# First loads of a two-block transformer kernel dealt to two DMA queues, and one split placed ahead of two sums

## The chip, the core and the metric

The kernel runs on one core of a Trainium2 chip: TensorE (PE) for matmuls, VectorE (DVE), ScalarE (ACT), GpSimd (POOL), SyncE (SP), and 16 DMA engines that the queues of SP, ACT and POOL share. The metric is device time in microseconds (us), the median of several executions; one further execution was profiled.

## The reference

256 tokens of width 1024 pass through a first block (modulated FFN, token mixer, modulated FFN) and a second block of two layers. What matters here is the first block's opening:

```python
cond = jax.nn.silu(c)                                  # c: 1024 values
mod = cond @ w_ada[l] + b_ada[l]                       # w_ada: 1024 x 9216
sh1, sc1, gt1, sh2, sc2, gt2, sh3, sc3, gt3 = jnp.split(mod, 9, axis=-1)
u = modulate(rmsnorm(h, g_norm_ffn1[l]), sh1, sc1)     # x * (1 + sc1) + sh1
h = h + 0.5 * gt1 * swiglu(u, w_ffn1_in[l], w_ffn1_out[l])
```

So before the first real matmul the kernel needs `x`, the shift columns of `w_ada` (block 0, 1024 x 1024), its scale columns (block 1, the same size), a bias and a gain vector, and the first unit of `w_ffn1_in`. All is float32; matmuls take each operand as a sum of two float16 parts (`hi` + `lo`), three products each.

## The kernel before

**Weights.** Weights of the matmuls come in units of 1 MiB (128 partitions x 2048 floats) into a ring `raw` of six slots. ACT makes `whi` of a unit (L444), DVE makes `wlo` (L469, `lo_part`), PE then multiplies (L750). Units 0 and 1 are the two halves of the first FFN chunk (its a and its b side). SP issues the units (`load`, L561); from unit 2 on it first waits until block 0 of the modulation is used up, since slots 2 to 5 hold that block until then.

**The opening.** Each modulation block comes in four pieces of 1 MiB, `j` = 0 to 3, of two row tiles each. DVE multiplies the pieces 0, 1 and 2 by `cond` and sums them (`ada_first_sums`, six sums, L2343 and L2345); PE takes piece 3 directly (`ada_direct`, L1054) and adds DVE's sums over partitions (`ada_ones`, L1060). ACT issues block 0 (pieces in the order 0, 3, 1, 2), the two halves of `x` (L1858) and, when `cond` is made, block 1 (L542). SP issues `c`, an identity matrix, a 204 KB table of constants (`small`, L565), 17 vectors of gains and biases (L575) and two rows of `b_ada` (L578), then positions, sinks and a router bias (L579 to L582), and units 0 and 1. The constants' table, the 17 vectors and the two bias rows count on one semaphore, `stack_in`; each counts 16, so 20 loads make 320.

**Who waits.** PE works in program order: `c` transposed (L1045), `ada_direct(0)`, then a wait for all 20 loads of `stack_in`, the transposes of the vectors and biases (L1067, L1068), then a wait for DVE's six sums, `ada_ones(0)` (L1060), 12 matmuls on zeros that keep the engine busy (`stay_warm`, L902), the transposes of the normalised `x` (L882), `ada_direct(1)` with two such matmuls before each pair, five more, `ada_ones(1)` (first 4 columns after sum 12, the other 4 after sum 13), five more, four matmuls that open the output banks (L822), five fillers (L853), and only then the first product of unit 0 (L750). ACT waits for `stack_in` too, before the mean squares of `x` (L1739). DVE waits for PE's two vector transposes between the sums of block 0 and those of block 1. After the sums of block 1 DVE makes `wlo` of unit 0, then the shift and scale columns (L2488 to L2495), from which ACT and DVE make `uhi` and `ulo`, the other operand of unit 0.

The order of all this is written out by hand; each queue issues in program order.

Of the kernel before, what the change touches and what calls it, by code (L numbers as in the profile page):

```python
# [27 lines left out]
D = 1024  # L28
# [5 lines left out]
RING = 6  # L34
# [6 lines left out]
HALF = 512  # L41
# [133 lines left out]
def build(nc, a, out):  # L175
    small_d, b1_d, b2_d = a["const_small"], a["const_block1"], a["const_block2"]
    with ExitStack() as ctx:
        def sb(name, shape, dt=F32):
            return ctx.enter_context(nc.sbuf_tensor(name, shape, dt))

        def sem(name):
            return ctx.enter_context(nc.semaphore(name))


        raw = sb("raw", [P, RING, UNIT])
# [164 lines left out]
        raw_in = [sem(f"raw_in{i}") for i in range(RING)]  # L350
        hi_made, lo_made, used = sem("hi_made"), sem("lo_made"), sem("used")
# [80 lines left out]
        def size(u):  # L432
            return sizes.get(u.c, UNIT) if isinstance(u.turn, int) and u.turn == 0 else UNIT
# [26 lines left out]
        def lo_part(dve, u):  # L460

            if isinstance(u.turn, int) and u.c + RING * u.turn >= U_END:
                return
            if ada_index(u) is not None:
                ada_unit_sums(dve, u, ada_index(u))
                return
            n = size(u)
            dve.wait_ge(hi_made, u.count(1))
            dve.scalar_tensor_tensor(out=wlo[:, u.slot, 0:n], in0=raw[:, u.slot, 0:n], scalar=SW,  # L469
                                     in1=whi[:, u.slot, 0:n], op0=ALU.mult, op1=ALU.subtract).then_inc(lo_made, 1)  # L470
# [51 lines left out]
        ffn1 = Phase(U_FFN1, 0, FFN_CHUNKS, ffn_src(a["w_ffn1_in"][0], a["w_ffn1_out"][0]))  # L522
# [10 lines left out]
        def ada_index(u):  # L533

            if isinstance(u.turn, int) and u.turn == 0 and u.c - U_MIX in ADA_POS:
                return ADA_POS.index(u.c - U_MIX)
            return None

        def ada_first(eng, b):

            for j in (0, 3, 1, 2):
                eng.dma_start(first_w[b][j], w_ada[:, 2 * j:2 * j + 2, b * D:(b + 1) * D]).then_inc(ada_in[b][j], 16)  # L542

        def ada_block(eng, b):

# [8 lines left out]
        @block.sync  # L554
        def _(sp):
            def load(u, src):
                if isinstance(u.turn, int) and u.c + RING * u.turn >= U_END:
                    return
                sp.wait_ge(lo_made, u.count(1 - RING))
                k, n = src.shape[1], src.shape[2]  # L560
                sp.dma_start(raw[:, u.slot, 0:k * n].rearrange("p (k n) -> p k n", k=k), src).then_inc(raw_in[u.slot], 16)  # L561

            sp.dma_start(cstack[0:8, :], a["c"][0].rearrange("(r n) -> r n", n=P)).then_inc(const_in, 16)
            sp.dma_start(small[:, 0:P], small_d[:, 0:P]).then_inc(const_in, 16)
            sp.dma_start(small[:, P:C_SMALL], small_d[:, P:C_SMALL]).then_inc(stack_in, 16)  # L565
            rows = [(V_G1, a["g_norm_ffn1"][0]), (V_G2, a["g_norm_mix"][0]),
                    (V_G3, a["g_norm_ffn2"][0]), (V_GF, a["g_final"])]
            for l in range(LAYERS):
                rows += [(V_LN1G + 8 * l, a["ln1_g_2"][l]), (V_LN1B + 8 * l, a["ln1_b_2"][l]),
                         (V_LN2G + 8 * l, a["ln2_g_2"][l]), (V_LN2B + 8 * l, a["ln2_b_2"][l]),  # L570
                         (V_QN + 3 * l, a["mla_q_norm_w_2"][l]), (V_KVN + 2 * l, a["mla_kv_norm_w_2"][l])]
            rows.append((V_PS, a["pool_scale"][0]))
            for r, v in rows:
                v = v.rearrange("(r n) -> r n", n=P)
                sp.dma_start(vstack[r:r + v.shape[0], :], v).then_inc(stack_in, 16)  # L575
            for r, m in ((B_SH1, M_SH1), (B_SH3, M_SH3)):
                v = a["b_ada"][0, m:m + 2 * D].rearrange("(r n) -> r n", n=P)
                sp.dma_start(bstack[r:r + 16, :], v).then_inc(stack_in, 16)  # L578
            sp.dma_start(posi, a["positions"][0].partition_broadcast(P)).then_inc(rows_in, 16)  # L579
            sp.dma_start(sinks[:, :], a["swa_sinks_2"].rearrange("l h -> (l h)").partition_broadcast(P)).then_inc(rows_in, 16)  # L580

            sp.dma_start(rbias[:, :], a["router_bias_2"].partition_broadcast(P)).then_inc(rows_in, 16)  # L582

            def phase(ph):
                load(Unit(ph.u0), ph.src("a", 0))
                load(Unit(ph.u0 + 1), ph.src("b", 0))
                if ph is ffn1:
                    sp.wait_ge(ada_sum, 6)
                    sp.wait_ge(ada_pe, 1)

                def step(c, u, par):
                    load(u, ph.src("a", c))
                    load(u + 1, ph.src("b", c))
                    load(u + 2, ph.src("o", c - 1))
                steps(sp, ph, step)
                load(Unit(ph.u0 + 3 * ph.n - 1), ph.src("o", ph.n - 1))

            phase(ffn1)
            for i in range(N_MIX):
                load(Unit(U_MIX + i), sources[U_MIX + i])  # L600
            phase(ffn2)
            for l in range(LAYERS):
                for i in range(N_LMIX):
                    load(Unit(U_L + N_L * l + i), sources[U_L + N_L * l + i])
                units, wholes = moe_units(l)

                def load_whole(c):
                    i = WHOLE.index(c)
                    if i >= 2:
                        sp.wait_ge(whole_used, N_WHOLE * l + i - 1)  # L610
                    sp.dma_start(whole[i % 2].rearrange("p (k n) -> p k n", k=2), wholes[c]).then_inc(whole_in[i % 2], 16)

                for i, src in enumerate(units):
                    if i == 4:
                        sp.wait_ge(ret_t, l + 1)
                        sp.wait_ge(p_made, 4 + 12 * (l + 1))
                        load_whole(WHOLE[0])
                        sp.wait_ge(ret_o, 4 * (l + 1))
                        load_whole(WHOLE[1])
                    load(Unit(U_L + N_L * l + N_LMIX + i), src)  # L620
                    for c in WHOLE[2:]:
                        if MOE_ORDER[i] == ("in", c + 2, 1):
                            load_whole(c)
                for c in WHOLE[2:]:
                    if c + 2 >= EXPERTS:
                        load_whole(c)
            for t in range(TT):
                for hf in range(2):
                    c = slice(hf * HALF, (hf + 1) * HALF)
                    sp.wait_ge(x_new, 12 + 2 * t + hf + 1)  # L630
                    sp.dma_start(out[0, t * P:(t + 1) * P, c], x[:, t, c]).then_inc(out_done, 16)
            sp.wait_ge(out_done, 64)
# [1090 lines left out]
        def _(act):  # L1723
# [129 lines left out]
                act.activation(gate_sig[i], ps[:, 5 + i % 2, :], ACT.Copy, scale=1.0 / S).then_inc(proj_out, 1)  # L1853


            ada_first(act, 0)
            for t in range(TT):
                act.dma_start(x[:, t, :], a["x"][0, t * P:(t + 1) * P, :]).then_inc(x_in, 16)  # L1858
            act.wait_ge(vec_t, 1)
            act.activation(cond[:, :], ps[:, 3, 0:8], ACT.Silu).then_inc(cond_made, 1)  # L1860
            ada_first(act, 1)
            act.wait_ge(used, RING)
            act.wait_ge(stack_in, 16 * 20)
            rms_first()
# [15 lines left out]
            for i in range(10):  # L1880
                u = Unit(U_MIX + IN1_POS[i])
# [360 lines left out]
        def _(dve):  # L2242
# [89 lines left out]
            def ada_first_sums(b, cuts, ks=range(6)):  # L2332

                for k in ks:
                    if k % 2 == 0:
                        dve.wait_ge(ada_in[b][k // 2], 16)
                    edges = cuts if k == 5 else (0, D)
                    if k:
                        dve.wait_ge(ada_sum, 6 * b + k)
                    for c0, c1 in zip(edges, edges[1:]):  # L2340
                        v, w = acc1[:, b * D + c0:b * D + c1], first_w[b][k // 2][:, k % 2, c0:c1]
                        if k == 0:
                            ins = dve.tensor_scalar(v, w, cond[:, 0:1], None, ALU.mult)  # L2343
                        else:
                            ins = dve.scalar_tensor_tensor(out=v, in0=w, scalar=cond[:, k:k + 1], in1=v,  # L2345
                                                           op0=ALU.mult, op1=ALU.add)
                        ins.then_inc(ada_sum, 1)
# [127 lines left out]
                n_step[0] += 2  # L2475
            ada_first_sums(1, (0, HALF, D), range(2))
            rms_xn(0)
            ada_first_sums(1, (0, HALF, D), range(2, 6))
            lo_part(dve, Unit(0))

            def mod_columns(i, ps_sh, ps_sc, g):

# [498 lines left out]
```

## Time and profile before

| | |
|---|---|
| median of 3 runs | 1118.47 us (1117.57 to 1119.99) |
| profiled execution | 1117.76 us, span 1116.0 us |
| PE busy | 1077.0 us, 97% of the span |
| DVE / ACT / POOL busy | 78% / 57% / 8% |
| chain that ended last | PE 81%, DVE 10%, ACT 4%, DMA 3% |
| DMA in the first four slices of 27.9 us | 340, 370, 371, 373 GB/s, busy tenths 9 9 9 9 |
| PE in the first slice | 6 tenths; 9 tenths in all others but the last (6) |

The span runs from the first instruction to the last; the profiled execution's own time has 1.76 us around it. The chain is followed back from the last instruction: a share in it is time that something really waited for. Busy time alone says little: PE's first slice holds fillers too.

### The profile page before, as it was taken

To read this page: it belongs to the slowest core of one execution; us is meant where nothing else is said; L and a number is where in the kernel's file an instruction comes from. 1 tells how busy PE (TensorE), PEld (TensorE's weight loads), DVE (VectorE), ACT (ScalarE), POOL (GpSimd) and SP (SyncE) were. 2 spreads that over 40 slices of the span, in tenths; PEclk is the share of its full clock that TensorE was granted. 3 is DMA by queue.
4 is the path that set the end of the run, shared out by engine and by line. 5 is a ranking of instruction groups with operands and counts; after the bars stand their busy time and mean duration, and the time that the engine had idled before them with its cause. 6 is when DMAs were issued, how large, how long until landed. Compare 5 with 4: busy or idle time off the path is not lost.

```text
span 1116.0 us, 24969 instructions
## 1 busy us (share of the span) xinstructions
PE 1077.0 (97%) x10736; PEld 819.0 (73%) x10736; DVE 874.7 (78%) x1130; ACT 633.1 (57%) x792; POOL 90.5 (8%) x104
## 2 busy tenths in 40 slices
PE   6999999999999999999999999999999999999996
PEld 5677777688788577777778785877758877597773
DVE  4789699788787885554667967999966886799994
ACT  1544344463466554444367555877755755687771
POOL 1114621043000110000000000000000000000000
PEclk9899999999999999999999999999999999999998
DMA  9999799754556578554546226499993523579981
GB/s 340 370 371 373 278 316 359 247 177 160 189 187 229 195 254 305 194 184 167 175 143 237 94 77 231 184 378 416 414 315 107 183 89 108 222 263 396 416 363 39
DMA packets 134717, 271.94 MB, mean 244 GB/s; under 512 B 9428, under 2 KB 98104, under 8 KB 126296
## 3 DMA queue, kind: packets, MB, share of 16 engines
q1 hardware_dynamic: 124248, 231.79, 58.1%
q0 software_dynamic: 7904, 29.25, 7.3%
q10 hardware_dynamic: 2464, 9.44, 2.2%
q8 instruction: 77, 1.26, 0.5%
q14 instruction: 24, 0.20, 0.0%
HBM read 269.41 MB, written 1.05 MB: 242 GB/s over the span
## 4 chain that ended last, share of the span: by engine, by line
PE 81%; DVE 10%; ACT 4%; DMA 3%; issue 2%; ACTq 0%; DVEq 0%; SPq 0%
PE ps L750 67%; PE ps L1625 3%; DVE wlo L469 3%; DMA area<-in_w_ada_dram 2%; PE ps L1673 1%; PE ps L892 1%; PE ps L902 1%; DVE area L2841 1%; PE ps L910 1%; PE ps L1278 1%; PE ps L1247 1%; PE ps L1087 1%; DVE bnst L2282 1%; ACT area L1776 1%; PE ps L1308 1%
## 5 line engine op out<-in xcount | busy, mean ns | idle before, releaser
L469 DVE SCALAR_TENSOR_TENSOR wlo<-raw,whi 128x2048 f16<-128x2048 f32 (+4 forms) x212 | 466.0, 2231 | 36.6 <-ACT whi L444 36.0
L444 ACT ACTIVATE whi<-raw 128x2048 f16<-128x2048 f32 (+4 forms) x212 | 385.2, 1850 | 25.8 <-DMA raw<-in_w_ffn_in_dram 10.2
L750 PE MATMUL ps<-uhi,whi 128*128 128x256 f16 (+2 forms) x1328 | 329.6, 260 | 2.2 <-DVE ulo L2308 2.0
L750 PE MATMUL ps<-uhi,wlo 128*128 128x256 f16 (+2 forms) x1328 | 329.4, 260 | 0.0
L750 PE MATMUL ps<-ulo,whi 128*128 128x256 f16 (+2 forms) x1328 | 329.4, 260 | 0.0
L750 PE MATMUL ps<-whi,hreg 128*128 128x512 f16 (+1 forms) x656 | 205.0, 381 | 0.0
L750 PE MATMUL ps<-area,whi 128*128 128x96 f16 (+2 forms) x2168 | 155.0, 210 | 0.0
L750 PEld LDWEIGHTS ps<-area,whi 128*128 128x128 f16 (+2 forms) x2168 | 145.4, 99 | 11.7 <-issue 5.6
L750 PE MATMUL ps<-area,wlo 128*128 128x96 f16 (+2 forms) x1084 | 149.4, 210 | 0.0
L750 PEld LDWEIGHTS ps<-uhi,whi 128*128 128x128 f16 (+1 forms) x1328 | 130.3, 98 | 23.5 <-issue 8.9
L750 PEld LDWEIGHTS ps<-ulo,whi 128*128 128x128 f16 (+1 forms) x1328 | 130.2, 98 | 15.6 <-issue 1.9
L750 PEld LDWEIGHTS ps<-uhi,wlo 128*128 128x128 f16 (+1 forms) x1328 | 130.1, 98 | 11.5
L750 PE MATMUL ps<-wlo,hreg 128*128 128x512 f16 (+1 forms) x328 | 124.9, 381 | 0.0
L750 PEld LDWEIGHTS ps<-whi,hreg 128*128 128x128 f16 (+1 forms) x656 | 68.9, 105 | 70.6 <-issue 3.0
L750 PEld LDWEIGHTS ps<-area,wlo 128*128 128x128 f16 (+2 forms) x1084 | 107.3, 99 | 0.0
L2359 DVE SCALAR_TENSOR_TENSOR area<-area,cond 128x512 f32 (+1 forms) x94 | 72.0, 766 | 10.7 <-DMA area<-in_w_ada_dram 7.5
L1796 ACT ACTIVATE hreg<-ps 128x512 f32<-128x512 f32 x22 | 13.2, 599 | 117.1 <-PE ps L750 117.1
L750 PEld LDWEIGHTS ps<-wlo,hreg 128*128 128x128 f16 (+1 forms) x328 | 34.5, 105 | 33.5 <-issue 2.1
L2325 DVE SCALAR_TENSOR_TENSOR hreg<-ps,hreg 128x512 f32<-128x512 f32 x22 | 15.1, 688 | 46.2 <-ACT hreg L1796 46.2
L549 POOL DMA_DIRECT2D area<-in_w_ada_dram x48 | 35.0, 729 | 161.8 <-DVE area L2359 129.6
L1798 ACT ACTIVATE hreg<-hreg 128x512 f16<-128x512 f32 x22 | 13.9, 632 | 56.2 <-DVE hreg L2325 56.2
L750 PE MATMUL ps<-whi,uhi 128*128 128x256 f16 (+2 forms) x176 | 38.8, 244 | 2.0 <-DVE ulo L2310 2.0
(358 smaller groups left out, 1324.6 us busy)
## 6 DMA issues: line engine op xcount, KB each, us to landing
raw<-in_exp_w_gate_up_dram SPq DMA_DIRECT2D x64, 1024.0 KB, 8.4
raw<-in_w_ffn_in_dram SPq DMA_DIRECT2D x44, 1024.0 KB, 7.5
raw<-in_w_in_dram SPq DMA_DIRECT2D x34, 1024.0 KB, 7.0
area<-in_w_ada_dram POOLq DMA_DIRECT2D x48, 512.0 KB, 7.1
raw<-in_w_ffn_out_dram SPq DMA_DIRECT2D x22, 1024.0 KB, 7.6
raw<-in_exp_w_down_dram SPq DMA_DIRECT2D x22, 1024.0 KB, 9.2
raw<-in_w_out_dram SPq DMA_DIRECT2D x12, 1024.0 KB, 4.9
x<-in_exp_w_down_dram SPq DMA_DIRECT2D x6, 1024.0 KB, 10.1
```

What stands on the lines that cost most here:

```text
L444: act.activation(whi[:, u.slot, 0:n], raw[:, u.slot, 0:n], ACT.Copy, scale=SW)\
L469: dve.scalar_tensor_tensor(out=wlo[:, u.slot, 0:n], in0=raw[:, u.slot, 0:n], scalar=SW, in1=whi[:, u.slot, 0:n], op0=ALU.mult, op1=ALU.sub ...
L549: eng.dma_start(aring[:, j, :, :], w_ada[:, 2 * j:2 * j + 2, c0:c0 + ADA_BLOCK]).then_inc(ada_late[j], 16)
L750: last = pe.matmul(o, st, mv, start=start and i == 0, stop=stop and i == 2, skip_group_check=True)
L892: ins = pe.transpose(ps[:, 4 + 2 * t + k // 4, (k % 4) * P:(k % 4 + 1) * P], xn[:, t, k * P:(k + 1) * P], ident)
L902: pe.matmul(ps[:, bank, :], ident16, zeros16[:, :], start=True, stop=True)
L910: pe.matmul(o, st[:, k, xs], res_one, start=k % 4 == 0 and i == 0, stop=False, skip_group_check=True)
L1625: last = pe.matmul(ps[0:SLOTS, 6 + n, :], e_whole[i % 4][:, f * SLOTS:(f + 1) * SLOTS], whole[i % 2][:, f * D + n * HALF:f * D + (n + 1) * ...
L1796: act.activation(s_act, ps[:, 4 + 2 * par, :], ACT.Silu, scale=1.0 / S).then_inc(silu_made, 1)
L1798: act.activation(hhi[:, par, :], h_f32, ACT.Copy).then_inc(h_hi, 1)
L2325: dve.scalar_tensor_tensor(out=h_f32, in0=ps[:, 5 + 2 * par, :], scalar=SX / S, in1=s_act, op0=ALU.mult, op1=ALU.mult).then_inc(h_made, 1)
L2359: ins = dve.scalar_tensor_tensor(out=v, in0=w, scalar=cond[:, k:k + 1], in1=v, op0=ALU.mult, op1=ALU.add)
```

## The change

`ada_first` takes the list of pieces to issue. Of each modulation block, pieces 0 and 1 stay on ACT, and pieces 3 and 2 go to SP. On SP, block 0's two pieces stand right behind `c` and the identity, ahead of the constants' table and the vectors; unit 0 and block 1's two pieces stand behind the bias rows and ahead of positions, sinks and router bias. Unit 1 moves from SP to ACT, behind its pieces of block 1. On DVE, `wlo` of unit 0 moves ahead of the last two sums of block 1 (the three instructions of rows 4 and 5).

```diff
-        def ada_first(eng, b):
-            for j in (0, 3, 1, 2):
+        def ada_first(eng, b, js):
+            for j in js:
                 eng.dma_start(first_w[b][j], w_ada[:, 2 * j:2 * j + 2, b * D:(b + 1) * D]).then_inc(ada_in[b][j], 16)
+        def fetch(eng, u, src):
+            k, n = src.shape[1], src.shape[2]
+            eng.dma_start(raw[:, u.slot, 0:k * n].rearrange("p (k n) -> p k n", k=k), src).then_inc(raw_in[u.slot], 16)
...
             sp.dma_start(small[:, 0:P], small_d[:, 0:P]).then_inc(const_in, 16)
+            ada_first(sp, 0, (3, 2))
             sp.dma_start(small[:, P:C_SMALL], small_d[:, P:C_SMALL]).then_inc(stack_in, 16)
...
+            load(Unit(ffn1.u0), ffn1.src("a", 0))
+            ada_first(sp, 1, (3, 2))
             sp.dma_start(posi, a["positions"][0].partition_broadcast(P)).then_inc(rows_in, 16)
...
             def phase(ph):
-                load(Unit(ph.u0), ph.src("a", 0))
-                load(Unit(ph.u0 + 1), ph.src("b", 0))
                 if ph is ffn1:
                     sp.wait_ge(ada_sum, 6)
                     sp.wait_ge(ada_pe, 1)
+                else:
+                    load(Unit(ph.u0), ph.src("a", 0))
+                    load(Unit(ph.u0 + 1), ph.src("b", 0))
...
-            ada_first(act, 0)
+            ada_first(act, 0, (0, 1))
...
-            ada_first(act, 1)
+            ada_first(act, 1, (0, 1))
+            act.wait_ge(lo_made, Unit(ffn1.u0 + 1).count(1 - RING))
+            fetch(act, Unit(ffn1.u0 + 1), ffn1.src("b", 0))
             act.wait_ge(used, RING)
             act.wait_ge(stack_in, 16 * 20)
...
-            ada_first_sums(1, (0, HALF, D), range(2, 6))
+            ada_first_sums(1, (0, HALF, D), range(2, 4))
             lo_part(dve, Unit(0))
+            ada_first_sums(1, (0, HALF, D), range(4, 6))
```

SP's queue at the program's start. In the kernel before (`hreg` takes the vectors, `raw` and `area` take weights; lines as in that kernel):

```order
L563 DMA hreg<-in_c_dram 8x128
L564 DMA small<-in_const_small_dram 128x128
L565 DMA small<-in_const_small_dram 128x408
L575 DMA hreg<-in_g_norm_ffn_dram 8x128
...
L578 DMA hreg<-in_b_ada_dram 16x128 x2
L579 DMA gt<-in_positions_dram 128x256
L580 DMA sinks<-in_swa_sinks_dram 128x12
L582 DMA rbias<-in_router_bias_dram 128x16
L561 DMA raw<-in_w_ffn_in_dram 128x8x256 x2
```

The same place in the changed kernel (its lines are numbered a few higher):

```order
L567 DMA hreg<-in_c_dram 8x128
L568 DMA small<-in_const_small_dram 128x128
L542 DMA raw<-in_w_ada_dram 128x2x1024 x2
L570 DMA small<-in_const_small_dram 128x408
L580 DMA hreg<-in_g_norm_ffn_dram 8x128
...
L583 DMA hreg<-in_b_ada_dram 16x128 x2
L547 DMA raw<-in_w_ffn_in_dram 128x8x256
L542 DMA area<-in_w_ada_dram 128x2x1024 x2
L586 DMA gt<-in_positions_dram 128x256
L587 DMA sinks<-in_swa_sinks_dram 128x12
L589 DMA rbias<-in_router_bias_dram 128x16
```

Two pieces of `w_ada` now stand ahead of the 20 loads of `stack_in`, one weight unit and two more pieces ahead of the positions.

ACT's queue and engine at the program's start, in the kernel before (`x` is the input, `cond` the activated `c`):

```order
L542 DMA raw<-in_w_ada_dram 128x2x1024 x4
L1858 DMA x<-in_x_dram 128x1024 x2
L1860 ACT_TABLE_LOAD
L1860 ACTIVATE cond<-ps 128x8
L542 DMA area<-in_w_ada_dram 128x2x1024 x4
L1739 ACTIVATE xn,stat<-x 128x1024
```

And in the changed kernel:

```order
L542 DMA raw<-in_w_ada_dram 128x2x1024 x2
L1866 DMA x<-in_x_dram 128x1024 x2
L1868 ACT_TABLE_LOAD
L1868 ACTIVATE cond<-ps 128x8
L542 DMA area<-in_w_ada_dram 128x2x1024 x2
L547 DMA raw<-in_w_ffn_in_dram 128x8x256
L1747 ACTIVATE xn,stat<-x 128x1024
```

`x` now stands behind two pieces, not four, and the issue of unit 1 stands between `cond` and the mean squares.

DVE at the end of block 1's sums, in the kernel before (`area` holds the sums, `adacols` and `acol` the shift and scale columns):

```order
L2345 SCALAR_TENSOR_TENSOR area<-area,cond 128x1024 x3
L2345 SCALAR_TENSOR_TENSOR area<-area,cond 128x512 x2
L469 SCALAR_TENSOR_TENSOR wlo<-raw,whi 128x2048
L2488 SCALAR_TENSOR_TENSOR adacols<-ps,vecb 128x8
L2494 TENSOR_TENSOR acol<-ps,vec 128x8
```

And in the changed kernel:

```order
L2355 SCALAR_TENSOR_TENSOR area<-area,cond 128x1024 x2
L469 SCALAR_TENSOR_TENSOR wlo<-raw,whi 128x2048
L2355 SCALAR_TENSOR_TENSOR area<-area,cond 128x1024
L2355 SCALAR_TENSOR_TENSOR area<-area,cond 128x512 x2
L2499 SCALAR_TENSOR_TENSOR adacols<-ps,vecb 128x8
L2505 TENSOR_TENSOR acol<-ps,vec 128x8
```

`wlo` of unit 0 no longer stands between the last sum and the columns.

## Rows read from the trace of the kernel before

**Rows 1.** Chain that ended last, 0 to 130 us: start, us, what.

```profile
1.21 4.53 DMA small<-in_const_small_dram
...
7.62 26.44 DMA area<-in_w_ada_dram
...
38.22 0.71 issue
...
43.55 86.60 PE ps L750 x680
```

**Rows 2.** PE's waits, 0 to 240 us: waiter, releaser, total us, times, longest.

```profile
PE ps L1060 <- DVE area L2345: 2.2, 2, 1.3
PE ps L892 <- DVE xn L2276: 0.7, 1, 0.7
```

**Rows 3.** PE's timeline to 44 us: start, us, line, operation, count, idle before.

```profile
9.11 6.96 PE L1054 MATMUL ps<-cond,raw 128*128 128x1 f32 x32 [3.03 <-DMA raw<-in_w_ada_dram]
15.93 0.42 PE L1067 MATMUL ps<-small,hreg 108*128 108x108 f32 x1
...
17.94 3.57 PE L1060 MATMUL ps<-small,area 128*128 128x1 f32 x16 [1.34 <-DVE area L2345]
21.37 4.80 PE L902 MATMUL ps<-zeros,diag 128*128 128x512 f16 x12
26.01 1.91 PE L882 MATMUL ps<-small,xn 128*128 128x128 f32 x16
27.76 0.59 PE L902 MATMUL ps<-zeros,diag 128*128 128x512 f16 x2
...
34.10 1.24 PE L902 MATMUL ps<-zeros,diag 128*128 128x512 f16 x5
36.21 1.95 PE L1060 MATMUL ps<-small,area 128*128 128x1 f32 x16 [0.87 <-DVE area L2345]
...
39.42 1.89 PE L822 MATMUL ps<-zeros 1*128 1x512 f16 x4 [0.17 <-DVE acol L2495]
41.24 2.31 PE L853 MATMUL ps<-zeros,diag 128*128 128x512 f16 x5
43.35 0.42 PE L750 MATMUL ps<-uhi,whi 128*128 128x256 f16 x1
```

**Rows 4.** DMA packets per queue (q10 ACT's, q1 SP's), 8 to 12 us.

```profile
q10 hardware_dynamic: 395, 1.49, 97.6%
q1 hardware_dynamic: 169, 0.04, 5.4%
```

**Rows 5.** The same, 20 to 30 us: packets, MB, share of 16 engines.

```profile
q10 hardware_dynamic: 821, 3.17, 79.7%
q1 hardware_dynamic: 823, 0.84, 23.8%
```

**Rows 6.** DMA issues on SP's queue, 8 to 11 us.

```profile
8.16 0.78 SPq L578 DMA_DIRECT2D hreg<-in_b_ada_dram  x2
...
10.40 5.02 SPq L561 DMA_DIRECT2D raw<-in_w_ffn_in_dram  x2
```

**Rows 7.** Landings of those issues: size of one, us from issue to landing.

```profile
raw<-in_w_ffn_in_dram SPq DMA_DIRECT2D x1, 1024.0 KB, 23.2
gt<-in_positions_dram SPq DMA_DIRECT2D x1, 128.0 KB, 7.5
```

**Rows 8.** DVE's timeline, 12 to 40 us.

```profile
15.28 2.60 DVE L2345 SCALAR_TENSOR_TENSOR area<-raw,cond,area 128x1024 f32<-128x1024 f32 x2 [0.59 <-DMA raw<-in_w_ada_dram]
...
34.08 2.73 DVE L2345 SCALAR_TENSOR_TENSOR area<-area,cond 128x1024 f32<-128x1024 f32 x3 [2.14 <-DMA area<-in_w_ada_dram]
36.73 2.29 DVE L469 SCALAR_TENSOR_TENSOR wlo<-raw,whi 128x2048 f16<-128x2048 f32 x1
```

**Rows 9.** ACT's timeline to 44 us, one row of the mean squares.

```profile
19.36 1.06 ACT L1739 ACTIVATE xn<-x 128x1024 f32<-128x1024 f32 x1 [13.10 <-DMA x<-in_x_dram]
```

**Rows 10.** Busy time by stretch: PE, PEld, DVE, ACT, POOL, PEclk, DMA share, GB/s.

```profile
40.00:45.00 5.00, 5.00 (x17) 2.09 (x15) 4.30 (x8) 4.59 (x8) 0.35 (x1) 0.50 1.05 393
```

More of the change, by code:

```diff
@@ L559, in load @@
                 sp.wait_ge(lo_made, u.count(1 - RING))
-                k, n = src.shape[1], src.shape[2]
-                sp.dma_start(raw[:, u.slot, 0:k * n].rearrange("p (k n) -> p k n", k=k), src).then_inc(raw_in[u.slot], 16)
+                fetch(sp, u, src)
             sp.dma_start(cstack[0:8, :], a["c"][0].rearrange("(r n) -> r n", n=P)).then_inc(const_in, 16)
             sp.dma_start(small[:, 0:P], small_d[:, 0:P]).then_inc(const_in, 16)
+            ada_first(sp, 0, (3, 2))
             sp.dma_start(small[:, P:C_SMALL], small_d[:, P:C_SMALL]).then_inc(stack_in, 16)
```

## The prediction

> **What bounds the kernel now.** I read the chain of waits first, to find which part of the program the change can reach. It has a DMA piece of 26.44 us, the modulation weights, ending at 34.06, then two short pieces on DVE with 0.71 us of "issue" at 38.22, and from 43.55 on PE alone [rows 1]. PE's waits come next: up to 240 us, behind that opening, PE waits 0.7 us in all for another engine [rows 2]. So whatever moves PE's first product of unit 0 (43.35) moves the end by as much, and nothing later gives it back or adds to it.
>
> The third view is PE's own timeline of the opening [rows 3]. It looks like waiting for weights, but the reader is to see that PE has a fixed row of work there. From `ada_ones(0)` at 17.94 to the end of the five fillers at 34.10 + 1.24 = 35.34 there is no idle: 17.40 us of back-to-back work. Only then comes a wait of 0.87 for DVE's last sums, `ada_ones(1)` from 36.21, and, as the chain says, readiness at 38.22 for columns that DVE starts 0.71 later because it still makes `wlo` of unit 0 (36.73 + 2.29 = 39.02 [rows 8]). So two chains run side by side: the weights' (piece 2 of block 1 at 34.06, three part sums, 2.73) and PE's, which has 0.87 of slack. A gain on the weights alone is therefore capped at 0.87 + 0.71 = 1.58 us, unless `ada_ones(0)` starts sooner too.
>
> What starts `ada_ones(0)`? In program order PE first needs block 0's piece 3 (matmuls from 9.11 for 6.96), then all 20 loads of `stack_in` for the two transposes, then DVE's sixth sum (15.28 + 2.60 = 17.88 [rows 8]). In the kernel before, the transposes start at 15.93 with no idle, so the 20 loads had landed by then, and the sixth sum came last (1.34 idle) [rows 3].
>
> **The change, part by part.**
>
> *Two queues.* One queue alone keeps the DMA engines at 97.6% of their share, 395 packets in 4 us, 99 a microsecond [rows 4]; the page has 340 GB/s in the first slice and 370 in the next. So the second queue brings no bytes sooner; it only changes the order of landing. Where both queues are full, each passes the same number of packets, 821 against 823 in 10 us, although ACT's are 4 KB (3.17 MB) and SP's 1 KB (0.84 MB) [rows 5]: the engines take one of each in turn.
>
> *Block 0's pieces 3 and 2 ahead of the constants.* The identity lands at 5.74 as before [rows 1]. From about there each queue holds 512 packets of 4 KB: SP pieces 3 and 2, ACT piece 1 and `x`. 1024 packets at 99 a microsecond are 10.3 us, so piece 2 lands at about 16.0, and behind it on the same queue come the constants and the vectors. In the kernel before these 20 loads started behind the identity at 5.74 and landed not before 12 (in 8 to 12 us SP's queue passed 169 packets with only 0.04 MB, still the small rows [rows 4]) and not after 15.93. That is 6.3 to 10.2 us for the list, in part because SP issued it until 8.16 + 0.78 = 8.94 [rows 6]; the positions, issued next, landed 7.5 us later, about 16.5 [rows 7]. Now the whole list is issued long before its turn, but it still passes one small packet for each of ACT's. So `stack_in` is full between 22.3 and 26.2. ACT's 4 KB packets end at about 16.0 + 512 / 82 = 22.2 (82 a microsecond from rows 5) and what is left then passes faster, so I take 23.3, near the lower end.
>
> *What that starts late.* PE's two transposes and the step to `ada_ones(0)` took 17.94 - 15.93 - 1.34 = 0.67; so `ada_ones(0)` starts at 24.0 instead of 17.94: +6.1 us. Its 17.40 us of work follow unchanged, to 41.4, where DVE's sums are no longer what ends last: the 0.87 of idle go.
>
> *`wlo` ahead of the last sums.* The 0.71 go as well. In its new place `wlo` stands before sums that wait for piece 2, so it is hidden if unit 0 is there: unit 0 goes in turn with unit 1 (on ACT) behind the vectors, 2 MiB at the page's 370 GB/s, 5.7 us, to 29.0; `whi` then takes 2 us on ACT and `wlo` is made by about 34. If unit 0 came later, the two queued sums and PE's `ada_ones(1)` would wait behind it.
>
> *What else now has slack.* Block 1's piece 3 (29.0 + 256 / 99 = 31.6) is needed by PE at 24.0 + (27.76 - 17.94) = 33.8. Piece 2 lands at 34.2 to 35.6 (the last one before landed at 34.06 with about the same bytes moved); the three part sums end by 38.3, needed at 41.4. DVE's backlog behind the transposes, four sums of 1.3, `wlo` 2.3 and an allowance of 3 us for the normalised `x` and the vectors, ends at 35.2. The mean squares, 19.36 before [rows 9], now wait for `stack_in`; they led to the transposes of `x` 6.65 us later (26.01), so 30.0, needed at 32.1. Unit 1's issue on ACT can block that engine only while its queue is full, which ends before 23.3. Positions, sinks and router bias come 15 us later and are used after several modulation blocks. All these cost nothing while `stack_in` is as late as this; each would be next if it came 2 to 3 us sooner.
>
> *Sum.* +6.1 - 0.87 - 0.71 = +4.5 us. The profiled execution took 1117.76; 1122.3 us. It lies 0.7 below the median of the runs, so the range leans upwards. With the ends of the list's time the sum runs from +3.5 to +7.4.
>
> *Clock.* In 40 to 45 us PE's granted clock is 0.50, the 1.2 GHz level [rows 10]. Before it fell PE had idled 0.87 and done narrow matmuls. The five fillers at 41.24 took 2.31 there and 1.24 at 34.10 [rows 3]. Without the idle the clock may stay up: then the fillers give back 1.1, the four openers 0.8 at most, and `ulo` limits the rest: 1.6 us, 1120.7. If it falls a second time or later, into dense products, 1 to 2 us are added.
>
> *A rule weighed.* Rows 4 and 5 show one packet of each queue in turn, with the vectors' small rows among them. The Trainium skill, "DMA: Bandwidth & Descriptors", section "Queues, rings and completion order", says that an engine drains a whole packet, typically 9 to 17 descriptors, from one ring before it turns to the next. By that rule each vector would wait for a burst of ACT's packets; the trace disagrees, since 169 small packets passed beside 395 large ones.
>
> **Rivals.**
>
> *Faster: the small loads are not late.* If they slip between the weight pieces, DVE's sixth sum starts `ada_ones(0)` again: piece 2 at 16.0 + 2.6 = 18.6, against 17.88, so +0.7 - 1.58 = -0.9, 1116.9; with the clock kept up 1115.3. It needs `stack_in` before 18.8 to break even. For it: their bytes are few (0.3 MB). Against it: equal turns, and one queue in order, as the positions show, which landed behind the vectors. 8% for faster.
>
> *No change.* `stack_in` at about 21 (the list drains in 5 us) and the clock kept up: +2.2 - 1.6, about 1118.5; also the upper part of the case above. 13%.
>
> *Slower still.* The list takes its 10.2 us: 1125.2; or piece 3 of block 1 or the clock come last as well: 1124 to 1127. 6%.
>
> *Bursts.* By turns of 16 large packets, 16 x 16 / 99 = 2.6 us each, 17 vectors would be 44 us late: about 1160. Rows 4 speak against it; 1%.
>
> **How the numbers follow.** The forecast, small loads late on PE's path, has 72%: 1122.3, from 1119.8 to 1125. About 2.2 us, 0.2%, is what a measurement of this kernel can tell from no change: 1116.2 to 1120.7 around 1118.47. Faster 8%, same 13% (with the lower part of the forecast's range and a kept clock already in it), slower 79% (72 + 6 + 1). The range for 8 of 10 is 1118.0 to 1125.5: it leaves out the faster case and a little above.
>
> **What the profile would show.** PE's transposes of the vectors (the rows at 15.93) at 23 to 24, with some 7 us of idle before them put down to DMA; no idle before the second `ada_ones`; DVE's columns straight behind it, near 43.5; the first product of unit 0 at 47 to 48.5; ACT's mean squares at 23 rather than 19.36. PE waits behind that as few as before. The forecast is wrong if the transposes still start at 16 to 19, or if PE waits later for weights that it did not wait for.

## The result and the profile after

The changed kernel takes 1121.2 us (median of 20 runs, 1118.96 to 1124.69), the kernel before 1118.07 in the same comparison (20 runs). The ratio is 1.0036 with a 95% interval of 1.0026 to 1.0046, so 2.9 to 5.1 us more: slower, beyond the 0.2% that can be told from no change. The profiled execution took 1122.22 us (span 1120.4; before 1117.76 and 1116.0). In the ratios below one execution of "the split alone" is left out: it took 2855.23 us, the kernel's three others 1124.27 to 1124.67.

The chain that ended last, 0 to 130 us (start, us, what):

```profile
9.56 14.87 DMA hreg<-in_b_ada_dram
...
24.48 0.44 PE ps L1075
...
48.29 81.80 PE ps L758 x650
```

Before, the opening's long piece was a weight piece that landed at 34.06 [rows 1]. Now it is the list of small loads, ending at 9.56 + 14.87 = 24.43, and PE alone carries the chain from there. `hreg` is where the vectors are stacked; PE's transposes of them are L1075.

PE's waits, 0 to 240 us (waiter, releaser, total us, times, longest):

```profile
PE ps L1062 <- DMA raw<-in_w_ada_dram: 5.6, 1, 5.6
PE ps L1075 <- DMA hreg<-in_b_ada_dram: 5.5, 1, 5.5
PE ps L900 <- DVE xn L2286: 0.7, 1, 0.7
```

The two waits for DVE's sums, 2.2 us in all [rows 2], are gone. In their place stand 5.5 us for the vectors; the wait for piece 3 grew from 3.03 [rows 3] to 5.6. The 0.7 behind the opening is the same as before.

PE's timeline of the opening (start, us, line, operation, count, idle before), to be laid beside [rows 3]; lines moved by 8:

```profile
11.97 6.96 PE L1062 MATMUL ps<-cond,raw 128*128 128x1 f32 x32 [5.58 <-DMA raw<-in_w_ada_dram]
24.48 0.44 PE L1075 MATMUL ps<-small,hreg 108*128 108x108 f32 x1 [5.54 <-DMA hreg<-in_b_ada_dram]
25.09 3.57 PE L1068 MATMUL ps<-small,area 128*128 128x1 f32 x16
28.52 4.61 PE L910 MATMUL ps<-zeros,diag 128*128 128x512 f16 x12
...
41.06 1.24 PE L910 MATMUL ps<-zeros,diag 128*128 128x512 f16 x5
42.14 1.84 PE L1068 MATMUL ps<-small,area 128*128 128x1 f32 x16
...
45.98 2.31 PE L861 MATMUL ps<-zeros,diag 128*128 128x512 f16 x5
48.09 0.42 PE L758 MATMUL ps<-uhi,whi 128*128 128x256 f16 x1
```

From `ada_ones(0)` at 25.09 (17.94 before) the same row of work runs to `ada_ones(1)` at 42.14 without idle. The first product of unit 0 starts at 48.09 instead of 43.35: +4.74. Piece 3 comes 2.9 us later (11.97 against 9.11), but behind it stand 5.54 us of idle: piece 3 decided nothing.

DVE in the same stretch:

```profile
32.37 2.29 DVE L469 SCALAR_TENSOR_TENSOR wlo<-raw,whi 128x2048 f16<-128x2048 f32 x1
34.58 2.73 DVE L2355 SCALAR_TENSOR_TENSOR area<-area,cond 128x1024 f32<-128x1024 f32 x3
...
44.09 0.17 DVE L2499 SCALAR_TENSOR_TENSOR adacols<-ps,vecb 128x8 f32<-128x8 f32 x1 [6.79 <-PE ps L1068]
```

The split of unit 0 now stands ahead of the last sums, at 32.37 instead of 36.73 [rows 8]. DVE then idles 6.79 us in front of the columns, waiting for PE. Whatever the change gained on DVE lies under that wait.

PE's granted clock in two stretches (the columns are those of [rows 10]: busy us and count of PE, PEld, DVE, ACT, POOL, then PEclk, DMA share, GB/s):

```profile
40.00:45.00 5.00, 5.00 (x37) 3.58 (x35) 0.41 (x3) 0.43 (x1) 2.93 (x4) 1.00 1.06 378
45.00:50.00 5.00, 5.00 (x22) 2.48 (x22) 4.16 (x8) 4.58 (x9) 0.00 (x0) 0.66 1.07 376
```

The clock still fell to the 1.2 GHz level, though PE had not idled since 24.48: by the trace's record of the clock from 45.98 to 49.39, for 3.41 us, against 39.20 to 46.03, 6.83 us, before. Fewer of the first products ran at the low level, so a thousand products on PE is 4.07 us late, not 4.74 (175.82 against 171.75), and the span ends 4.4 us later.

### The profile page after: what moved, and what is told of

The parts are those of the page before. It is cut to its first block, busy times and chain, and to the rows that moved or that the text cites. A ratio compares the mean times of both kernels' runs of the same rounds, so it can differ in the third digit from the quotient of the medians.

```text
span 1120.4 us, 24969 instructions
## 1 busy us (share of the span) xinstructions
PE 1074.7 (96%) x10736; PEld 819.2 (73%) x10736; DVE 874.9 (78%) x1130; ACT 632.2 (56%) x792; POOL 90.1 (8%) x104
## 4 chain that ended last, share of the span: by engine, by line
PE 82%; DVE 9%; ACT 4%; issue 2%; DMA 1%; SPq 1%; DVEq 0%; ACTq 0%
PE ps L758 67%; PE ps L1633 3%; DVE wlo L469 3%; PE ps L910 2%; DMA hreg<-in_b_ada_dram 1%; PE ps L1681 1%; PE ps L900 1%; DVE area L2852 1%; PE ps L918 1%; PE ps L1286 1%; PE ps L1255 1%; PE ps L1095 1%; DVE bnst L2292 1%; ACT area L1784 1%; PE ps L1316 1%
```

## The experiments

Two theories stood against each other. Mine: the 20 small loads (`stack_in`) stand behind two weight pieces on one queue, and that alone costs the time. The rival: the new place of the split, or the late piece 3, costs it. Later a second question came up: whether an earlier start reaches the end at all. "First product" below is PE's first product of unit 0 in each profile; it stands at 43.35 before and 48.09 after. "Columns" is DVE's first instruction on the shift and scale columns, 38.93 before [rows 1] and 44.09 after. It is the better measure of what the loads do: in the kernel before, the changed kernel, the kernel with piece 3 on ACT as well and "the split alone" the five fillers behind the columns ran at the 1.2 GHz level (2.31 us), in the other six at 2.4 GHz (1.25 us), so a difference between first products holds the clock too (in "the split alone" the columns hold some of it as well). Ratios are to the kernel before.

| kernel | columns, us | first product, us | ratio [95%] |
|---|---|---|---|
| changed kernel | 44.09 | 48.09 | 1.0036 [1.0026, 1.0046] |
| block 0 on ACT alone | 38.81 | 41.79 | 1.0017 [1.0000, 1.0035] |
| only block 0 dealt | 45.05 | 48.02 | 1.0054 [1.0035, 1.0073] |
| block 0 on ACT, piece 3 of block 1 on ACT | 38.34 | 43.46 | 1.0002 [0.9991, 1.0013] |
| changed, split back | 44.45 | 47.42 | 1.0044 [1.0031, 1.0057] |
| split alone | 43.73 | 49.62 | 1.0067 [1.0050, 1.0084] |
| changed, vectors twice | 47.59 | 50.56 | 1.0069 [1.0054, 1.0084] |
| unit 1 last | 37.39 | 40.36 | 0.9996 [0.9986, 1.0005] |
| small loads first | 47.53 | 50.50 | 1.0061 [1.0046, 1.0077] |

**Block 0 on ACT alone**, from the changed kernel:

```diff
-            ada_first(sp, 0, (3, 2))
...
-            ada_first(act, 0, (0, 1))
+            ada_first(act, 0, (0, 3, 1, 2))
```

> Undoes one part: block 0's pieces 3 and 2 go back to ACT (order 0, 3, 1, 2), so SP's queue again starts with the 20 small loads; block 1 and units 0 and 1 stay dealt as in the changed kernel, and the DVE order stays. Theory (small loads behind two weight pieces start PE's fixed row late): the transposes of the vectors are back near 16.0, ada_ones(0) at 17.9, and the loss of 4 us is gone. But block 1's piece 3 now stands behind unit 0 on SP and lands near 29 to 29.5, while PE comes for it at 27.8: 1.2 to 1.7 us of new wait, which eats the 0.87 + 0.71 that the change frees. First product near 43.3, time within 0.1% of the kernel before. Rival (the loss comes from block 1's pieces and the units on two queues): still 3 to 4 us slower than before.

PE's timeline:

```profile
16.00 0.42 PE L1074 MATMUL ps<-small,hreg 108*128 108x108 f32 x1
...
17.65 3.57 PE L1067 MATMUL ps<-small,area 128*128 128x1 f32 x16 [0.99 <-DVE area L2354]
...
29.43 0.61 PE L909 MATMUL ps<-zeros,diag 128*128 128x512 f16 x2 [1.74 <-DMA area<-in_w_ada_dram]
```

The vectors' transposes are back at 16.00 and DVE's sums release `ada_ones(0)` again, so the late start is gone. Of the time about half went: 1.0017, with an interval that still overlaps that of the changed kernel. What is late next is piece 3 of block 1, 1.74 us, and the columns are where they were (38.81; 38.93 before). That the first product came 1.56 us earlier is almost all the clock's doing, which stayed at 2.4 GHz here, and it did not last: in this execution the clock was low for 6.83 us from 209.70, in the kernel before for 3.41 from 213.28, and over that stretch PE went from 1.49 us ahead to 0.18 behind.

**Only block 0 dealt**, from the kernel before:

```diff
-        def ada_first(eng, b):
+        def ada_first(eng, b, js=(0, 3, 1, 2)):
-            for j in (0, 3, 1, 2):
+            for j in js:
...
+            ada_first(sp, 0, (3, 2))
...
-            ada_first(act, 0)
+            ada_first(act, 0, (0, 1))
```

> One part alone on the kernel before: only block 0 is dealt to two queues (pieces 3 and 2 on SP ahead of the small loads); block 1 stays on ACT, units 0 and 1 stay on SP behind the positions, DVE's order is that of before. Theory: the 20 small loads land at 24 to 25.5 (ACT's queue now carries 4 KB packets all the time), ada_ones(0) starts at 25 to 26, first product at 48 to 49; 4 to 5 us slower than before, the whole loss of the change or a little more. DVE's late split costs nothing here since PE's row ends after it. Rival (block 1 and the units): no slower than before.

PE's timeline:

```profile
24.63 0.44 PE L1068 MATMUL ps<-small,hreg 108*128 108x108 f32 x1 [6.06 <-DMA hreg<-in_b_ada_dram]
...
25.24 3.57 PE L1061 MATMUL ps<-small,area 128*128 128x1 f32 x16
```

This one edit gives the late transposes (24.63; 24.48 in the changed kernel), the late first product (48.02), and a ratio whose interval takes in the 1.0036 of the changed kernel. Together with the kernel above, which takes back this edit alone, the cause of the late start is shown from both sides. For the time, the kernel above gives back only about half; the next one, which also leaves block 0 on ACT and removes the new wait for piece 3, has no loss left (1.0002).

**Piece 3 of block 1 on ACT as well**, from "block 0 on ACT alone", to take away its 1.74 us:

```diff
-            ada_first(sp, 1, (3, 2))
+            ada_first(sp, 1, (1, 2))
...
-            ada_first(act, 1, (0, 1))
+            ada_first(act, 1, (0, 3))
```

> As the kernel with block 0 back on ACT, but block 1 dealt so that ACT carries pieces 0 and 3 and SP, behind unit 0, pieces 1 and 2. Theory: PE's row starts at 17.9 as before; piece 3 lands near 26, before PE comes for it at 27.8; piece 1 near 29.5, piece 2 near 34; no idle of 0.87 before ada_ones(1), no split ahead of the columns: columns at 37.4 instead of 38.9, first product 1 to 1.6 us earlier than in the kernel before, 1116.5 to 1117.5 if the clock does as before, up to 1.6 us less if it does not fall. Rival (only the clock or the bytes matter): the same time as the kernel before.

A miss: nothing was gained. DVE's timeline, then PE's wait:

```profile
31.96 2.28 DVE L469 SCALAR_TENSOR_TENSOR wlo<-raw,whi 128x2048 f16<-128x2048 f32 x1
34.16 2.73 DVE L2354 SCALAR_TENSOR_TENSOR area<-area,cond 128x1024 f32<-128x1024 f32 x3
38.34 0.17 DVE L2498 SCALAR_TENSOR_TENSOR adacols<-ps,vecb 128x8 f32<-128x8 f32 x1 [1.45 <-PE ps L1067]
```

```profile
36.28 1.95 PE L1067 MATMUL ps<-small,area 128*128 128x1 f32 x16 [1.24 <-DVE area L2354]
```

The wait only moved, from 1.74 for piece 3 to 1.24 for the last sums. Piece 2, the last, landed at 33.70, where it was at 34.06 in the kernel before: another order on the queues did not bring the last bytes much sooner, because the same bytes, two weight units among them, go ahead of them (with one unit less ahead, in "unit 1 last" below, it landed at 31.05). The split's new place has a part in it: the last sums start at 34.16, behind the split, and not at 33.70.

**The split back behind the sums**, from the changed kernel:

```diff
-            ada_first_sums(1, (0, HALF, D), range(2, 4))
+            ada_first_sums(1, (0, HALF, D), range(2, 6))
             lo_part(dve, Unit(0))
-            ada_first_sums(1, (0, HALF, D), range(4, 6))
```

> The changed kernel with DVE's order of before: the split of unit 0 behind the last sums again. Theory: DVE waits 6.8 us for ada_ones(1) in the changed kernel, so the split (2.3 us) fits in that wait: same time as the changed kernel within 0.1%, columns at 44.1, first product at 48.1. Rival (the new place of the split is itself a cost or a gain on the path): 0.7 us or more of difference in the time of the columns.

DVE's timeline:

```profile
36.44 2.28 DVE L469 SCALAR_TENSOR_TENSOR wlo<-raw,whi 128x2048 f16<-128x2048 f32 x1
44.45 0.17 DVE L2498 SCALAR_TENSOR_TENSOR adacols<-ps,vecb 128x8 f32<-128x8 f32 x1 [5.72 <-PE ps L1068]
```

The time stays that of the changed kernel. With PE this late, DVE waits 5.72 us in front of the columns even with the split in its old place: that part of the change is worth nothing beside the other. (The first product, 0.7 us earlier than in the changed kernel, is the clock's: the columns come 0.4 later.)

**The split alone**, the opposite edit in the kernel before:

```diff
-            ada_first_sums(1, (0, HALF, D), range(2, 6))
+            ada_first_sums(1, (0, HALF, D), range(2, 4))
             lo_part(dve, Unit(0))
+            ada_first_sums(1, (0, HALF, D), range(4, 6))
```

> One part alone on the kernel before: only DVE's split of unit 0 goes ahead of the last sums of block 1; all loads as before. Theory: unit 0 lands at 33.6 there, so whi ends at 35.6 and the split at 37.9; the last sums, whose piece landed at 34.1, queue behind it and end at 40.6 instead of 36.8; columns near 41.6 instead of 38.9, first product 2.5 to 3 us later, 2.5 to 3.5 us slower than before (PE's longer idle keeps its clock at the lower level). The move is free only together with the earlier unit 0. Rival (the split's place matters only for the columns): 0.7 us faster.

Slower as expected, but by 7.5 us (5.6 to 9.4), more than twice the size. DVE's timeline, then PE's:

```profile
35.71 2.29 DVE L469 SCALAR_TENSOR_TENSOR wlo<-raw,whi 128x2048 f16<-128x2048 f32 x1 [3.52 <-ACT whi L444]
37.92 2.73 DVE L2345 SCALAR_TENSOR_TENSOR area<-area,cond 128x1024 f32<-128x1024 f32 x3
```

```profile
40.04 3.57 PE L1060 MATMUL ps<-small,area 128*128 128x1 f32 x16 [4.79 <-DVE area L2345]
43.48 2.29 PE L902 MATMUL ps<-zeros,diag 128*128 128x512 f16 x5
```

Unit 0 comes too late for this order. The split waits 3.52 us for `whi`, the sums queue behind it, and PE's wait grows from 0.87 to 4.79. The part that I had reckoned too small is the clock: it stood at the 1.2 GHz level from 37.96 to 51.61, 13.65 us, so the 16 matmuls that took 1.95 before took 3.57. In the changed kernel this order is harmless: unit 0 was also moved ahead (29.10), and the last sums end at 34.58 + 2.73 = 37.31, long before PE comes for them at 42.14.

**The vectors twice**, from the changed kernel: each of the 17 vectors is loaded a second time into unused space, so the list grows by 0.05 MB; the waits count 37 loads.

```diff
-                sp.dma_start(vstack[r:r + v.shape[0], :], v).then_inc(stack_in, 16)
+                for part in (vstack, hreg[:, 896:896 + P]):
+                    sp.dma_start(part[r:r + v.shape[0], :], v).then_inc(stack_in, 16)
```

> The changed kernel with each of the 17 vectors loaded twice (the second time into a scrap area), 37 loads on stack_in instead of 20; only 0.05 MB more. Theory (each small packet takes a turn, and its load's count another): 34 more turns on the most loaded DMA engine. ACT's 4 KB packets end near 23, so these turns stand beside unit 1's 1 KB packets, 0.07 us each: the transposes start 2 to 3 us later, at 26.5 to 27.5, first product at 50 to 51, 2 to 3 us slower than the changed kernel. If the turns still stood beside 4 KB packets it would be 6 us. Rival (bytes count, not turns): 0.15 us.

PE's timeline:

```profile
27.61 0.44 PE L1076 MATMUL ps<-small,hreg 108*128 108x108 f32 x1 [8.76 <-DMA hreg<-in_b_ada_dram]
```

The transposes start 3.1 us later than in the changed kernel, a little more than expected, for bytes that at the profile's 370 GB/s would take 0.14. So a small load does not pay for its bytes. That it pays for turns, and not a fixed price of its own, is read from the packet counts further down: they go by what stands on the other queue.

**Unit 1 last**, from the kernel with piece 3 on ACT as well: unit 1 stands on SP behind block 1's pieces, so the last piece has one unit less ahead of it.

```diff
+            load(Unit(ffn1.u0 + 1), ffn1.src("b", 0))
...
-            act.wait_ge(lo_made, Unit(ffn1.u0 + 1).count(1 - RING))
-            fetch(act, Unit(ffn1.u0 + 1), ffn1.src("b", 0))
```

> The kernel with piece 3 of block 1 on ACT, and unit 1 issued on SP behind pieces 1 and 2 of block 1 instead of on ACT, where it took turns with them. Theory (two chains bound the opening, PE's row and the last piece with DVE's three sums; the earlier variant's 1.24 us of idle before ada_ones(1) was the second): piece 2 lands at 31.5 to 32.3 instead of 33.7, the sums end by 35, PE's row ends at 35.0, no idle; columns at 37.1 to 37.4 against 38.9 in the kernel before, so 1.5 us faster than the kernel before with the clock equal (about 0.1%), and no wait for unit 1 later. Rival (the last piece lands no sooner whoever takes turns with it): columns at 38.3 as in the earlier variant, no change.

The opening did what was asked: no idle in front of `ada_ones(1)`, columns at 37.39, 1.54 us earlier than before, first product at 40.36, 3.0 us earlier. The other 1.45 are the clock's, which stayed at 2.4 GHz in this opening: from the columns to the first product 2.97 us, 4.42 before. The time did not follow. PE's timeline around 195 us, where one FFN chunk ends and the next begins, in this kernel and then in the kernel before:

```profile
194.46 0.38 PE L758 MATMUL ps<-whi,hreg 128*128 128x512 f16 x1
196.78 0.27 PE L758 MATMUL ps<-uhi,whi 128*128 128x256 f16 x1 [1.94 <-issue]
```

```profile
197.59 0.38 PE L750 MATMUL ps<-whi,hreg 128*128 128x512 f16 x1
197.94 0.27 PE L750 MATMUL ps<-uhi,whi 128*128 128x256 f16 x1
```

At the end of the chunk PE is still 197.59 - 194.46 = 3.13 us ahead. The next chunk begins only 1.16 ahead, behind 1.94 us of idle that the kernel before does not have. DVE's product of this chunk, in this kernel and then in the kernel before:

```profile
194.36 0.68 DVE L2333 SCALAR_TENSOR_TENSOR hreg<-ps,hreg 128x512 f32<-128x512 f32 x1
```

```profile
195.52 0.68 DVE L2325 SCALAR_TENSOR_TENSOR hreg<-ps,hreg 128x512 f32<-128x512 f32 x1
```

DVE came to it without idle and is ahead by the same 1.16 us (the release itself is put down to "issue", so that PE's wait is DVE's is read from this agreement). DVE's lead was no larger at its first product of this kind (54.79, 55.97 before), and there the rows name what held it: a weight unit of `w_ffn_out`, for which ACT waits. ACT in this kernel, then in the kernel before:

```profile
50.64 1.91 ACT L444 ACTIVATE whi<-raw 128x2048 f16<-128x2048 f32 x1 [2.23 <-DMA raw<-in_w_ffn_out_dram]
```

```profile
49.88 1.91 ACT L444 ACTIVATE whi<-raw 128x2048 f16<-128x2048 f32 x1 [0.69 <-DMA raw<-in_w_ffn_out_dram]
```

The unit landed at 50.62, 49.85 before: no sooner, so an earlier start only waits longer for it. DVE then waited 1.81 us for ACT's `whi`, and its lead stayed at 1.1 to 1.2 us from there to 195. That its lead is set there is read from the rows; no run moved this unit alone. DVE was busy 124.4 of the 140 us from 60 to 200 in both kernels. Then the clock took more: in this execution it was low for 6.83 us from 210.29, in the kernel before for 3.41 from 213.28, and behind that PE is 0.5 us late. The other executions were not profiled, but their clock is on record: at a mean granted clock of 0.993 five executions of this kernel took 1116.3 us on average and seven of the kernel before 1116.3, at 0.994 three of each 1116.0. So no lower mean clock hides a gain there; where in them it went is not shown.

**Small loads first**, from the changed kernel: SP's two pieces of block 0 behind the 20 small loads.

```diff
-            ada_first(sp, 0, (3, 2))
...
+            ada_first(sp, 0, (3, 2))
             load(Unit(ffn1.u0), ffn1.src("a", 0))
```

> The changed kernel with the 20 small loads back ahead of block 0's pieces 3 and 2 on SP, all else as in the changed kernel. Theory (one queue in order, equal turns): the small loads land at 14.5 to 15.1 as in the kernel before, but the two pieces now stand behind them: piece 3 at 19 to 20, so PE's ada_direct(0) runs from there for 7 us, the transposes start at 26 to 27, ada_ones(0) at 27 to 28; first product at 50 to 51, 5.5 to 7 us slower than before. Dealing block 0 is then bad in either order. Rival (only the small loads matter, the pieces have slack): ada_ones(0) at 18 to 20 and the loss gone.

PE's timeline:

```profile
20.03 6.96 PE L1062 MATMUL ps<-cond,raw 128*128 128x1 f32 x32 [13.59 <-DMA raw<-in_w_ada_dram]
26.85 0.42 PE L1075 MATMUL ps<-small,hreg 108*128 108x108 f32 x1
27.44 3.57 PE L1068 MATMUL ps<-small,area 128*128 128x1 f32 x16
```

The vectors were there in time (14.77), but piece 3 then waits behind the list, and `ada_ones(0)` starts at 27.44, later still. Dealing block 0 to SP's queue costs time in both orders tried.

## Why the prediction was right, and where not

Forecast 1122.3 us, 4.5 above the profiled execution; measured 1121.2, by the ratio 4.0 above the kernel before (2.9 to 5.1), and 4.46 in the profiled execution.

*No bytes sooner with a second queue: right.* The last piece of block 1 landed at 34.21 (34.06 before; 34.2 to 35.6 predicted), unit 0 at 29.10 (29.0), piece 3 of block 1 at 31.66 (31.6).

*Turns of one packet: right.* Packets of ACT's queue (q10) and SP's (q1) in the changed kernel, 16 to 22 us (packets, MB, share of 16 engines):

```profile
q10 hardware_dynamic: 531, 1.96, 83.5%
q1 hardware_dynamic: 530, 0.39, 20.4%
```

Equal counts again, while SP moves a fifth of ACT's bytes; [rows 4] alone would not show it (395 against 169, with SP still issuing the list). From 22 to 25 us, when nearly all of ACT's packets are of 1 KB, the counts are 501 and 507 in 3 us: nearly twice as many turns in the same time. Equal bursts would give equal counts as well. What rules them out is the time of the small loads: 20 of them landed within 7.65 us (16.78 to 24.43), and 17 more cost 3.1 us (0.18 each), where the burst rival has 2.6 us for each. The Trainium skill, "DMA: Bandwidth & Descriptors", section "Queues, rings and completion order", has the engine turn between queues only after a whole packet of typically 9 to 17 descriptors. The times here disagree with bursts of that size.

*The list late: right, mis-sized by 1.1 us.* The prediction had piece 2 at 16.0 and the list at 23.3; they landed at 16.78 and 24.43. Of the 1.1, 0.8 lies in piece 2: the identity landed at 6.05 and not at 5.74 as before (PE's first transpose starts at 6.10, 5.78 before), and the 1024 packets then took 10.73 us, not 10.3. The other 0.3 lies in the list itself. So `ada_ones(0)` moved by +7.15, not +6.1.

*The 17.40 us of PE work unchanged: nearly.* By the same measure, to the end of the fillers at 41.06 + 1.24 = 42.30, it took 17.21. `ada_ones(1)` starts 0.16 before that end, so 17.05 behind `ada_ones(0)`. The 0.87 of idle behind it went, as predicted: 7.15 - 0.35 - 0.87 = 5.93 for `ada_ones(1)`.

*The 0.71 behind `wlo`: gone as a wait, but not by the new place.* With the split back in its old place the columns still waited for PE. The columns moved from 38.93 (38.22 + 0.71 [rows 1]) to 44.09, +5.16, and the first product by +4.74, beside +4.5 forecast.

*The clock: an open term that came out small.* It might stay up (-1.6) or fall again (+1 to 2). It fell for half as long, which gave back 0.4 us between the columns and the first product (4.00 us, 4.42 before) and 0.7 behind it. Of the reasons given, idle and narrow matmuls, the traces bear out idle in part: in the three kernels with idle right in front of `ada_ones(1)` (0.87 before, 1.24 in the kernel with piece 3 on ACT as well, 4.79 in "the split alone") the clock was low in the opening for 6.83, 6.83 and 13.65 us, and in six of the seven without it it stayed up. But in the changed kernel it fell at 45.98 with no idle in 20 us, and 1.74 us of idle, further ahead, did not bring it down in "block 0 on ACT alone". The narrow matmuls stand in all ten kernels. With one profile of each, what decides it stays open.

*How near the number came: in part luck.* The list was taken 1.1 us too early and 0.4 came up behind the opening; the row of work came out 0.35 shorter and the clock, for which the sum had no term, gave back 1.1. These errors cancel.

*What had slack: right.* No other wait came up in the opening, and 0.7 us of PE waits behind it stayed 0.7. Of the signs, the idle before the transposes was 5.54 us and not some 7, because piece 3, which had no time of its own in the prediction, kept PE busy to about 19.

*"Nothing later gives it back or adds to it": half wrong.* A delay goes through to the end; that was the case here, and so the forecast held (4.07 us a thousand products on, 4.4 at the end). An earlier start does not: in "unit 1 last" 1.54 us at the columns and 3.0 at the first product became 0.5 us in the comparison, with no change inside its interval. That PE waited for nothing in [rows 2] did not mean that it bounds the kernel alone. DVE and the weights behind it stood close: with PE 3.13 us earlier, DVE was only 1.16 earlier, because a weight unit landed no sooner. My rival "faster, 1115.3" counted an earlier start in full; in "unit 1 last", where it came, it did not reach the end.

## What to carry to other kernels

Where queues take turns by packets, a list of small loads must not stand behind bulk pieces, and bulk pieces on the critical path must not stand behind a list of small loads; the order on each queue is to be checked for the smallest load that an engine waits for, not only for the largest. A second queue on DMA engines that are already full only deals the bytes in another order. Before work goes into an earlier start, look at the second chain, here DVE behind a weight unit, and ask whether the same edit moves it as well: a delay cost about its whole length here, a gain at most what both chains gained.

## What the runs showed of the hardware

- A load of a few 512-byte rows costs turns. From 17.5 to 20 us SP's queue passed 226 packets in the changed kernel and ACT's 222, nearly all of ACT's of 4 KB. Of SP's 226, 147 carried data and 79 were of 4 bytes, by their size the semaphore writes. The counts are equal only with these in, so by this reading a semaphore write takes a turn of its own. Seventeen such loads more made 3.1 us.
- A wait of PE can cost more than its length through the clock: in "the split alone" `ada_ones(1)` started 3.8 us later (40.04 against 36.21) and the first product 6.3 us later (49.62 against 43.35), with 13.65 us at the 1.2 GHz level.
- The granted clock fell in some executions and not in others at like work: in "only block 0 dealt" it stayed at 2.4 GHz through the whole opening, in the changed kernel, with PE's same row of work, it fell for 3.41 us.
- A piece lands in sixteen parts, each counted on its semaphore, and one can hold up the whole. In the kernel before, fifteen parts of block 1's last piece had landed by 32.65, the last at 34.06, and the sums and PE's 0.87 us of idle hang on that one. A 16 KB packet of the instruction queue (q8) took 1.04 us from 30.29. Such a packet goes with a late last part in "the split alone" (33.09, then 34.18) and the kernel with piece 3 on ACT as well (32.75, then 33.70) too, but not in "unit 1 last" (30.70, then 31.05). That it is the cause is not shown: the records do not name the DMA engine.
